# Hybrid encoder layer with hierarchical MoE: output projection in two passes over depth

## What is computed

```
p = rmsnorm(x, norm_mix) @ w_in                      # 2048 x 6400
y = concat[ rwkv7(pA), band_attention(pB), diff_attention(pC), short_conv(pD) ]
x = x + y @ w_out                                    # 2048 x 2048
x = x + hier_moe(rmsnorm(x, norm_ffn))               # 4 groups x 8 experts, hidden 256
return rmsnorm(x, norm_final)
```

## Time and profile before

| | |
|---|---|
| Time, median of 3 runs | 940.85 us (940.47 to 941.32) |
| The profiled execution: its own time, its span | 940.73 us, 938.8 us |
| Granted TensorE clock, mean | 0.926 |
| Busy: TensorE | 787.3 us (84%) |
| Busy: VectorE, ScalarE, GpSimd | 432.1, 280.6, 73.5 us |
| HBM read, written | 280.37 MB, 4.22 MB |
| Chain of waits: TensorE, DMA | 59%, 33% |

### The profile page before, as it was taken

How to read it: one execution, slowest core, us unless ns; L and a number is a source line. 1 busy time by engine, 2 the same in 40 slices (tenths; PEclk the granted TensorE clock), 3 DMA queues, 4 the chain that set the end, 5 groups by cost and what they waited for, 6 DMA issues and landing times.

```text
span 938.8 us, 18498 instructions
## 1 busy us (share of the span) xinstructions
PE 787.3 (84%) x8182; PEld 634.4 (68%) x8182; DVE 432.1 (46%) x709; ACT 280.6 (30%) x458; POOL 73.5 (8%) x79
## 2 busy tenths in 40 slices
PE   7999999999999999999999774686646856559654
PEld 7999999999999999888877452353523534236322
DVE  6758947654676576854552513113231122311403
ACT  6455543433355666455510101000010000100014
POOL 3110003241000100600000000000000000000002
PEclk9999999999999999999999978797887978979878
DMA  9695544334344545999899999999999999999995
GB/s 302 208 284 159 177 134 137 120 110 135 108 147 153 148 147 180 349 347 365 287 341 404 427 427 429 427 426 428 427 427 427 427 429 426 426 428 427 427 403 203
DMA packets 84655, 285.83 MB, mean 304 GB/s; under 512 B 3818, under 2 KB 55284, under 8 KB 72156
## 3 DMA queue, kind: packets, MB, share of 16 engines
q1 hardware_dynamic: 82304, 278.93, 77.0%
q0 software_dynamic: 1568, 4.02, 1.7%
q10 hardware_dynamic: 700, 1.65, 0.5%
HBM read 280.37 MB, written 4.22 MB: 303 GB/s over the span
## 4 chain that ended last, share of the span: by engine, by line
PE 59%; DMA 33%; DVE 3%; ACT 2%; issue 1%; SPq 1%; POOL 1%; ACTq 0%; POOLq 0%; DVEq 0%
PE bank L1046 26%; DMA arena<-in_expert_w_up 12%; DMA arena<-in_expert_w_down 10%; DMA arena<-in_expert_w_gate 9%; PE bank L1510 8%; PE bank L1590 3%; PE bank L1063 3%; PE bank L1065 3%; PE bank L1064 3%; PE bank L965 2%; PE bank L1475 2%; DMA arena<-in_norm_final 1%; PE bank L1209 1%; DVE ring_r L1715 1%; PE bank L1016 1%
## 5 line engine op out<-in xcount | busy, mean ns | idle before, releaser
L1046 PE MATMUL bank<-xTr,hi 128*128 128x256 f32 x1280 | 235.7, 286 | 0.3 <-DVE ring_r L1715 0.2
L1510 PE MATMUL bank<-arena 128*32 128x256 f32 x2048 | 144.0, 449 | 104.5 <-DMA arena<-in_expert_w_up 60.8
L1046 PEld LDWEIGHTS bank<-xTr,hi 128*128 128x128 f32 x1280 | 199.2, 192 | 5.4 <-issue 3.3
L1715 DVE TENSOR_TENSOR ring_r<-arena,hi 128x1024 fp32r<-128x1024 f32 x132 | 161.9, 1236 | 88.0 <-ACT hi L654 85.5
L1510 PEld LDWEIGHTS bank<-arena 128*32 128x32 f32 x2048 | 80.3, 129 | 165.8 <-issue 138.4
L1046 PE MATMUL bank<-xTr,ring_r 128*128 128x256 f32 x640 | 181.0, 283 | 0.0
L654 ACT ACTIVATE hi<-arena 128x1024 fp32r<-128x1024 f32 x132 | 138.9, 1062 | 111.5 <-PE bank L1046 84.1
L1046 PEld LDWEIGHTS bank<-xTr,ring_r 128*128 128x128 f32 x640 | 122.7, 192 | 0.0
L2149 DVE TENSOR_TENSOR arena<-arena,bank 128x512 f32<-128x512 f32 x56 | 57.8, 1092 | 75.2 <-PE bank L1486 75.2
L895 ACT ACTIVATE g<-bank,coef 128x256 f32<-128x256 f32 x8 | 3.8, 473 | 256.0 <-PE bank L1510 256.0
L1590 PE MATMUL bank<-arena,const 128*32 128x512 f32 x448 | 54.6, 643 | 14.4 <-DMA arena<-in_expert_w_down 14.4
(11 more groups left out here) (338 smaller groups left out, 884.6 us busy)
## 6 DMA issues: line engine op xcount, KB each, us to landing
arena<-in_expert_w_gate SPq DMA_DIRECT2D x30, 2048.0 KB, 30.1
arena<-in_expert_w_up SPq DMA_DIRECT2D x29, 2048.0 KB, 31.8
arena<-in_w_in SPq DMA_DIRECT2D x50, 1024.0 KB, 5.3
arena<-in_expert_w_down SPq DMA_DIRECT2D x24, 2048.0 KB, 30.1
arena<-in_w_out SPq DMA_DIRECT2D x16, 1024.0 KB, 6.0
arena<-in_expert_w_down SPq DMA_DIRECT2D x16, 512.0 KB, 9.1
arena<-in_expert_w_down SPq DMA_DIRECT2D x8, 1024.0 KB, 15.6
arena<-in_expert_w_up SPq DMA_DIRECT2D x6, 1024.0 KB, 7.1
```

The lines of the kernel that those rows point to most:

```text
L1046: ins = MM(PJ[n % 2][:, h * U:(h + 1) * U], a, b, start=h + q + tt + k == 0, stop=h == 1 and q == 3 and tt == 3 and k == 2)
L1510: ins = MM(gu[slots_of(a), u * EH:(u + 1) * EH], xg[:, t, slots_of(a)], slot(NUQ * h + NCG * u + a)[:, t * EH:(t + 1) * EH], start=t == 0, ...
L1715: TT(ring_r[:, n % 2, q, :], ring[:, n % 2, q, :], hi[:, g % NHI, :].bitcast(f32), ALU.subtract).then_inc(s["lo_done"], 1)
```

## The change

The output projection runs over all four column blocks with the first half of the depth (8 granule tiles of `yTr`), then over all four with the second. The sum of the first pass is taken out of PSUM by ScalarE (`half_sums`) into the region `x2p`, permuted, and GpSimd adds it to the columns of x in `x2b` (signal `z_done`); the second pass starts a new sum in PSUM, and `residual` adds that. After the first pass the first half of both planes of `yTr` is free: SyncE then loads the first halves of units 8 and 9 there (`n == NU_IN + 5`) rather than quarters of them near the end; the parts that remain are issued after the last granules. The stores of `x2b` come later by the count of units. ScalarE copies the convolution in after one split fewer. Later waits on `x2p_done` and `z_done` have their counts raised. Between blocks of the second pass there are four granules rather than eight: two before the transposes, one, the logits, one.

```diff
--- before.py
+++ after.py
@@ -294,6 +294,8 @@
         LAND_LATER = 16 * NU_GROUP // NW_LATER
         used = [s[f"used{a}"] for a in range(NCG)]
         DOWN_PARTS = 3
+        NB = NU_OUT // 2
+        NG_B = NG_IN + 4 * NB
 
         def unit_slot(k, later):
 
@@ -391,7 +393,7 @@
                         dst = dst.rearrange("p (t c) -> p t c", t=KT // 2)
                         src = w_in_v[:, half * (KT // 2):(half + 1) * (KT // 2), order[n] * U:(order[n] + 1) * U]
                     else:
-                        nb, kh_ = (n - NU_IN) // 2, (n - NU_IN) % 2
+                        nb, kh_ = (n - NU_IN) % NB, (n - NU_IN) // NB
                         t0 = (2 * kh_ + half) * (KT // 4)
                         dst = dst.rearrange("p (t c) -> p t c", t=KT // 4)
                         src = w_out_v[:, t0:t0 + KT // 4, nb * 2 * U:(nb + 1) * 2 * U]
@@ -400,11 +402,14 @@
                     sp.wait_ge(s["sm_done"], sm_count(NBH + NCH - 1))
                     for nb in range(3):
                         sp.dma_start(x2b[nb], x_cols[:, :, nb * 512:(nb + 1) * 512]).then_inc(x2_ld[nb], 16)
-                if n in (NU_IN + 4, NU_IN + 6):
-                    store_x2((n - NU_IN) // 2 - 2)
-                if n == NU_IN + 6:
+                if n == NU_IN + 5:
+                    for k in (8, 9):
+                        moe_unit(0, k, part=halves[0])
+                if n in (NU_IN + 6, NU_IN + 7):
+                    store_x2(n - NU_IN - 6)
+                if n == NU_IN + 7:
                     sp.wait_ge(s["tx_ps"], 1)
-                    sp.wait_ge(s["x2p_done"], NM)
+                    sp.wait_ge(s["x2p_done"], NM * NB + NM)
                     sp.wait_ge(x2_st[0], 16)
                     sp.dma_start(x2b[0], x_cols[:, :, 3 * 512:4 * 512]).then_inc(x2_ld[0], 16)
                 if NU_IN < n < NU_IN + 6:
@@ -413,18 +418,17 @@
                     if n == NU_IN + 3:
                         sp.wait_ge(s["ylo_done"], YD1)
                     moe_unit(0, n - NU_IN - 1)
-            store_x2(2)
             for n in range(2):
                 sp.wait_ge(s["gran_used"], NG - 6 + 2 * n)
                 moe_unit(0, 5, part=halves[n])
+                if n == 0:
+                    store_x2(2)
+            for n in range(2):
+                sp.wait_ge(s["gran_used"], NG - 2 + 3 * n)
+                for k in (6, 7):
+                    moe_unit(0, k, part=halves[n])
                 for k in (8, 9):
-                    moe_unit(0, k, part=quarters[n])
-            sp.wait_ge(s["gran_used"], NG - 2)
-            for k in (6, 7):
-                moe_unit(0, k, part=halves[0])
-            sp.wait_ge(s["gran_used"], NG + 1)
-            for k in range(6, NW):
-                moe_unit(0, k, part=halves[1])
+                    moe_unit(0, k, part=quarters[2 + n])
             store_x2(3)
             for n in range(2):
                 sp.wait_ge(s["gate_quarter"], NCG * (n + 1))
@@ -564,6 +568,12 @@
                     step(G.tensor_tensor(c_[:, i], c_[:, i], h_[:, i], ALU.add))
             step(G.tensor_tensor(c_, c_, b_, ALU.mult), s["dconv0"])
 
+            for nb in range(NB):
+                pool.wait_ge(x2_ld[nb % 3], 16 * (nb // 3 + 1))
+                pool.wait_ge(s["x2p_done"], NM * (nb + 1))
+                for m in range(NM):
+                    t = x2b[nb % 3][:, m, :].rearrange("p (q t) -> p q t", t=KT)
+                    step(G.tensor_tensor(t, t, x2p[:, m, :, 32 * nb:32 * nb + 32].rearrange("p t q -> p q t"), ALU.add), s["z_done"])
             rsqrt(st[:, 0:NM])
             pool.wait_ge(s["route_done"], 1)
             more = pool.value_load(ovi[0:1, 0:1], min_val=0, max_val=1)
@@ -817,7 +827,7 @@
                 advance(2 if i < NCH else 1)
             out_high_c(NCH - 1)
             advance(1)
-            advance(NG_IN - pos["pe"] + 3)
+            advance(NG_IN + 2 - pos["pe"])
             act.wait_ge(s["dconv0"], 1)
             copy(yTr[:, 0, 12:14, :], Dq[:, 0, 1], s["yhi_done"])
             act.wait_ge(s["dconv1"], 1)
@@ -843,10 +853,20 @@
                     act.wait_ge(s["lgm_ps"], nb)
                 copy(xTn[0], PJ[0][:, :].rearrange("p (j n) -> p j n", j=2), s["txa_ev"])
 
+            def half_sums(nb):
+
+                act.wait_ge(s["gran_used"], NG_IN + 4 * (nb + 1))
+                for m in range(NM):
+                    copy(x2p[:, m, :, 32 * nb:32 * nb + 32], K[2 * (nb % 2) + m][:, :].rearrange("p (q t) -> p t q", t=KT),
+                         s["x2p_done"])
+
+            for nb in range(NB):
+                advance(NG_IN + 4 * (nb + 1) - pos["pe"])
+                half_sums(nb)
             for nb in range(3):
-                advance(NG_IN + 8 * (nb + 1) - pos["pe"])
+                advance(NG_B + 4 * (nb + 1) - pos["pe"])
                 square_block(nb)
-                advance(3)
+                advance(2)
                 logit_rows(nb)
                 advance(1)
                 rows_permuted(nb)
@@ -949,7 +969,7 @@
             act.wait_ge(s["rstd_done"], NRSTD)
             act.wait_ge(s["sq3_done"], 8)
             for n in range(4):
-                act.wait_ge(s["z_done"], max(3, n + 1))
+                act.wait_ge(s["z_done"], NM * NB + max(3, n + 1))
                 cols_ = slice(n * 512, (n + 1) * 512)
                 A_(x2n[:, 1, cols_], x2z[:, cols_], ACT.Copy, scale=st[:, 1:2]).then_inc(s["sq3_done"], 1)
                 if n % 2 == 1:
@@ -1048,9 +1068,14 @@
                 return ins
 
             def out_granule(n, q):
-                nb, kh_ = (n - NU_IN) // 2, (n - NU_IN) % 2
-                if kh_ == 0 and q == 0 and nb >= 2:
-                    pe.wait_ge(s["wo_ev"], 2 * (nb - 1))
+                nb, kh_ = (n - NU_IN) % NB, (n - NU_IN) // NB
+                if q == 0 and n == NU_IN + 1:
+                    pe.wait_ge(s["ylo_done"], YC)
+                if q == 0 and n >= NU_IN + 2:
+                    if kh_ == 0 or nb < 2:
+                        pe.wait_ge(s["x2p_done"], NM * (n - NU_IN - 1))
+                    else:
+                        pe.wait_ge(s["wo_ev"], NM * (nb - 1))
                 if nb == 0:
                     pe.wait_ge(s["ylo_done"], ((YA, YA, YB, YB), (YC, YC, YD0, YD1))[kh_][q])
                 g = 4 * n + q
@@ -1060,9 +1085,9 @@
                     o_, tok = K[2 * (nb % 2) + m][:, :], slice(m * P, (m + 1) * P)
                     for tt in range(2):
                         t = 8 * kh_ + 2 * q + tt
-                        MM(o_, yTr[:, 0, t, tok], wh[:, tt, :], start=t == 0, stop=False)
+                        MM(o_, yTr[:, 0, t, tok], wh[:, tt, :], start=t % 8 == 0, stop=False)
                         MM(o_, yTr[:, 1, t, tok], wh[:, tt, :], start=False, stop=False)
-                        ins = MM(o_, yTr[:, 0, t, tok], wl[:, tt, :], start=False, stop=t == KT - 1)
+                        ins = MM(o_, yTr[:, 0, t, tok], wl[:, tt, :], start=False, stop=t % 8 == 7)
                     if g == NG - 1 and m == 0:
                         ins.then_inc(s["gran_used"], 1)
                 return ins
@@ -1427,13 +1452,13 @@
                                  start=nb == 0 and j == 0, stop=False)
                 ins.then_inc(s["lgm_ps"], 1)
 
-            granules(NG_IN + 8 - pos["g"])
+            granules(NG_B + 4 - pos["g"])
             for nb in range(3):
-                granules(3)
+                granules(2)
                 rows_transpose(nb)
                 granules(1)
                 logits(nb)
-                granules(4)
+                granules(1)
             rows_transpose(3)
             for m in range(NM):
                 for j in range(4):
@@ -1608,7 +1633,7 @@
             keep_clock(1)
             pe.wait_ge(s["keys_done"], 1)
             pe.wait_ge(s["sel_done"], 1)
-            pe.wait_ge(s["x2p_done"], 8)
+            pe.wait_ge(s["x2p_done"], NM * NB + 8)
             gather(0, bank[0], x2p)
             gather(1, bank[1], x2p)
             for q in range(NQ):
@@ -2017,8 +2042,8 @@
 
             def residual(nb):
 
-                v.wait_ge(s["gran_used"], NG_IN + 8 * (nb + 1))
-                v.wait_ge(x2_ld[nb % 3], 16 * (nb // 3 + 1))
+                v.wait_ge(s["gran_used"], NG_B + 4 * (nb + 1))
+                v.wait_ge(s["z_done"], NM * (nb + 1))
                 for m in range(NM):
                     t = x2b[nb % 3][:, m, :]
                     step(TT(t, t, K[2 * (nb % 2) + m][:, :], ALU.add), s["wo_ev"])
@@ -2031,16 +2056,16 @@
                 step(V.tensor_copy(xTn[1], PJ[1][:, :].rearrange("p (j n) -> p j n", j=2)), s["txb_ev"])
 
             for nb in range(3):
-                split_lo(NG_IN + 8 * (nb + 1) + LEAD - pos["split"])
+                split_lo(NG_B + 4 * (nb + 1) + LEAD - pos["split"])
                 residual(nb)
                 if nb == 0:
                     v.wait_ge(par2_ld, 16 * 6)
                     step(TT(rw, rw, gain_tp[:, :].unsqueeze(2).to_broadcast([P, KT, 36]), ALU.mult), s["rw_scaled"])
```

(7 more changed lines are left out.)

## The result

| | before | changed |
|---|---|---|
| Time, median | 941.09 us (940.47 to 941.39, 4 runs) | 949.30 us (946.97 to 951.66, 4 runs) |
| The profiled execution: its time, its span | 940.73, 938.8 us | 951.66, 949.8 us |
| Busy: TensorE | 787.3 us (84%) | 790.8 us (83%) |
| Busy: VectorE, ScalarE, GpSimd | 432.1, 280.6, 73.5 us | 438.1, 285.2, 89.0 us |
| Mean granted TensorE clock | 0.926 | 0.920 |

The ratio is 1.0088, 95% interval 1.0060 to 1.0116: the change makes the kernel slower by 5.6 to 10.9 us. The forecast was 942.0 us with a range up to 945.3.

What follows compares the result with a forecast made beforehand. TensorE was taken to bound the kernel until the projection's end, the weight stream afterwards, started by TensorE's first slot release. Terms -1.0 + 1.0 + 0.3 + 1.0 = +1.3 us on 940.73 gave 942.0 us, range 939.5 to 945.3.

Steps and rivals of the forecast that it cites:

- The frame: Whole kernel: end time is TensorE's first slot release, plus fixed bytes at 427 GB/s, plus an untouched tail.
- a release later than 496 us: First slot release after the projection: forecast at 493 to 495 us; later than 496 would show the prediction wrong.
- The expert bytes: Early 2 MiB of units 8 and 9: 4.9 us of transfer, hidden by the wait for TensorE, costed at 0.
- The start of the stream: First quarter load after the release: lands sooner in a nearly empty queue, gain 0 to 1.5 us, taken as -1.0.
- ScalarE's order: Start of projection: convolution copies one split earlier delay granule 5 on TensorE, +1.0 us (0.9 to 1.1).
- Half sums and adds in block 0: Projection, granules 7 and 8: ScalarE copies and GpSimd adds use up the reserve, 0 to 1.1 us, taken as +0.3.
- Rival 3: GpSimd's strided adds of 2.2 us or more exclude VectorE each time: 943.9 us, deciding from 2 us per add; 12%.
- The ring load behind the burst: Ring half behind 4 MiB of expert loads lands late, delaying block 0's logits 0.2 to 2.5 us, taken as +1.0.

Runs made afterwards that it cites:

- a4_spread: Changed kernel with ScalarE's convolution copies one split later and the early halves of units 8 and 9 issued one at a time: 940.54 us, ratio 1.0004.
- a3_both: Changed kernel with ScalarE's convolution copies one split later and the first halves of units 8 and 9 loaded late, about as before: 940.86 us, ratio 1.0002.
- c1_again: Changed kernel, unedited, run and profiled a second time: 948.17 us, ratio 1.0077.
- b4_price: Kernel before the change with 18 filler matmuls of 512 columns ahead of granule 6 of the output projection: 945.87 us, ratio 1.0057.
- c3_adds_late_full: Changed kernel with GpSimd's first add held until TensorE has used eight granules, early loads kept: 943.57 us, ratio 1.0035.
- b5: a2 with GpSimd's first add held until TensorE has used eight granules: 942.17 us, ratio 1.0016.
- c2: Changed kernel with filler matmuls ahead of granules 5 (5) and 6 (9) and the logits of block 0 (4): 945.41 us, ratio 1.0050.
- a1: Changed kernel with ScalarE's convolution copies one split later, as before the change: 941.71 us, ratio 1.0019.
- a2: Changed kernel with the first halves of units 8 and 9 loaded near the projection's end, about as before the change: 946.14 us, ratio 1.0053.
- b6: a2 with filler matmuls in place of the waits, 5 ahead of granule 5 and 9 ahead of granule 6: 945.03 us, ratio 1.0046.

## Why the prediction was wrong

**The frame held.** The time is the first release plus a fixed stream. The stream rows before and after are alike, and the shift of the release explains each kernel: delays of TensorE in the projection come out at the end one for one, or up to 1.2 us over (the profiled spans against the releases). The sign of a release later than 496 us, which the prediction had named as proof against it, is what came.

**The expert bytes, 0: right.** a4_spread and a3_both differ in these bytes and by 0.3 us. In the changed kernel no byte moves between 501.86 and 502.2 us, when the release comes: every slot is full, as the prediction had it.

**The start of the stream, -1.0: no gain.** In the changed kernel's profile the first quarter landed 3.9 us after its issue instead of 5.3, as the term has it. But in c1_again, the same kernel, it took 5.8 us, and in b4_price, whose bytes are those of before, 4.0: over all profiles 3.4 to 5.8 us. The quarter behind it, issued 0.37 us later, took 6.2 us as before, and the last load of the kernel is issued late by the whole shift (9.94 us for 9.92). The landing of one load was no gain of the stream; the term had to be 0, its lower bound.

**ScalarE's order, +1.0: right**, 1.19 us at the granule named, behind the engine named.

**Half sums and adds in block 0, +0.3 within 0 to 1.1: the first step that failed; measured 2.11 us.** The price of an add was in the bounds (3.50 us for two, 1.75 each). The price of the copies was too high: 1.21 us for a pair, near the lower end of 1.1 to 2.3, where the working took 2.2. With that the first add was to start at 399.3 us, when VectorE had both low halves of y behind it, and the working looked for its effect only at granules 7 and 8: it had the low part of granule 6 done at 400.0 us, just ahead of TensorE (396.40 + 1.0 + 2.74 = 400.1 us). The add started at 397.82, 1.5 us earlier (1.0 us of this is the price, the rest an earlier start of the whole stage), 0.09 us ahead of the second low half (L2040). The first add held that one up by 1.34 us, the second add the low part of granule 6 by 1.2 us; the little reserve that was left turns 2.5 into 2.11 us. An operation that was cheaper than assumed cost time, because it changed who came first. Rival 3 had the exclusion and 2.2 us for it, but for adds of 2.2 us or more, deciding from 2 us on, and the price was 1.75; that its size agrees with the 2.11 us is luck. Its rule, from the Trainium skill (SBUF — State Buffer, Who interferes with whom), that a VectorE instruction with two SBUF inputs and a GpSimd one that reads SBUF exclude each other, agrees with the rows: 2.03 us with the add in progress, 0.69 us in c3_adds_late_full with GpSimd idle. b5 and c3 show that the start of the adds is the cause.

**The ring load behind the burst, +1.0 within 0.2 to 2.5: size right (1.23, 0.74, 0.68, 0.38 us in four runs), working wrong.** The prediction had the queue work through a backlog from 405 us on and deliver this half at 446.4. But the queue ran dry when TensorE stalled (share 0.01 from 406.1 us), and the load is issued only when TensorE frees its place. It then took 13.8, 13.3, 13.1, 13.2 and 12.9 us in the five kernels with the burst (the changed one, c1, c2, c3, a1), issued between 437.0 and 431.4 us. So the landing moves with TensorE, from 450.8 to 444.3 us; a backlog counted on from 405 us doesn't give it.

**TensorE's clock: no term at all, the second step that failed; it is about half of the loss.** The trace of before has 1.00 through the whole projection, and the working took the matmul at 0.228 us for granted. Behind the waits of 1.19 and 2.11 us it fell to 0.50 for 3.4 us in every profile in which both stood (after, c1, a2), behind the logits' waits for 6.8 and 3.4 us: 5.1 and 3.4 us of the releases' shifts of 9.9 and 7.6. By the medians the clock is 2.8 us of 7.3 (c1 less c2). b6 and c2 show that it is not the lateness but the idleness: the same delay with TensorE kept busy has 1.00. The Trainium skill (TensorE: Matmul & The Clock Gate, What's actually happening) says that a clock gate is set by how busy the engine has been recently; the trace agrees.

So of +9.6 us in the profiled execution: order 1.19 (forecast 1.0), adds 2.11 (0.3), logits 1.23 (1.0), clock 5.1 (none), start 0 (-1.0). Even without the clock the forecast was 3.2 us too low. With the adds' term alone put right it is 943.8 us, inside its range; with all the waits as they were and no gain at the start it is 945.3 us, the very end of the range, and c2_fill_all, which has the lateness without the clock, measured 945.41. The clock took the time the rest of the way, to 949.30.

**What stays open.** Why the second half-clock stretch is 3.4 us long in one run and 6.8 in another; that the nearly equal waits of c3_adds_late_full (0.45 + 0.23) leave the clock alone where those of c1_again (0.51 + 0.23) don't; where three of the four runs of b4_price lost 1 us more than the profiled one; and why eight of the releases come 0.3 to 0.8 us later than their sums. Leaving the 2 MiB out altogether was not tried. No version beat the kernel before: the best two equal it.

## What to carry to other kernels

Where TensorE works without a gap, ask of waits that stand near each other not only for their length but for a stretch at half clock behind them: here it cost 1.7 us behind 3.3 us of waits, 3.4 or 5.1 us behind 4.1 and 4.5 us, and nothing behind a single wait of 1.19 us. Matmuls that fill the waits took that part away. When an order is moved, follow the engines that share a resource with both the high and the low price of each new instruction: the cheap one can put it in front of a critical instruction that it would otherwise have followed. And memory that is free earlier gains nothing as long as the next request waits for another event; look first at what releases the request.

## What was new of the hardware

- TensorE's clock fell 0.2 to 0.9 us after the end of a wait of 2.1 us that followed one of 1.2 us and 3.0 us of work, stayed at 1.00 after a wait of 1.19 us alone, and in one run fell after only 0.51 + 0.23 us of waiting. Waits of the same length covered by matmuls left it alone.
- GpSimd's add of 128x512 with a strided input took 1.75 us (3.50 for two) to 2.3 us (4.63 for two in a1_plus3); ScalarE's copy of 128x512 from PSUM took 0.6 us.
- A 1 MiB load behind 4 MiB in the same queue landed 12.9 to 13.8 us after its issue; into a nearly empty queue it took 5.0 us.
- The first 512 KB load of the release landed after 3.4 to 5.8 us over all profiles, and in two profiles of one kernel after 3.9 and 5.8 us: a difference of 1 or 2 us in one landing says little.
